# A gated block inside a two-layer kernel: the u groups computed feature-major in the wide form, the spatial product with v stationary and one group behind

## The reference

```python
def chunk_mlp_mix(h, w_in, g_v, w_s, b_s, w_out):
    bsz, length, _ = h.shape
    z = jax.nn.gelu(h @ w_in)
    u, v = jnp.split(z, 2, axis=-1)
    v = rmsnorm_2(v, g_v).reshape(bsz, length // CHUNK_2, CHUNK_2, A_GROUPS, A_WIDTH // A_GROUPS)
    s = jnp.einsum('gpq,bnqgc->bnpgc', w_s, v) + b_s.T[None, None, :, :, None]
    return (u * s.reshape(bsz, length, A_WIDTH)) @ w_out
```

## Time and profile before

| | us |
|---|---|
| median of 3 runs (2377.48 to 2377.6) | 2377.57 |
| profiled execution | 2377.55 |
| its span, first to last instruction | 2375.8 |
| TensorE busy | 2361.4 (99%) |
| VectorE busy | 1675.4 (71%) |
| ScalarE busy | 1173.7 (49%) |
| HBM read | 546 MB, 231 GB/s |

### The profile page before, as it was taken

One profiled execution on the slowest core, in us unless ns is written; L12 is line 12 of the kernel. 1 busy time (PEld: TensorE's weight loads), 2 busy tenths in 40 slices (PEclk: granted clock), 3 DMA queues, 4 the chain that ended last, 5 costly groups with the idle time before them and its releaser, 6 DMA issues.

```text
span 2375.8 us, 31444 instructions
## 1 busy us (share of the span) xinstructions
PE 2361.4 (99%) x12340; PEld 2023.3 (85%) x12340; DVE 1675.4 (71%) x2216; ACT 1173.7 (49%) x1528; POOL 0.2 (0%) x4
## 2 busy tenths in 40 slices
PE   9999999999999999999999999999999999999998
PEld 9989888888888888888888888888888888888887
DVE  6775657877877877877667777556777567765776
ACT  5443545534534534556554433446655355544554
POOL 0000000000000000000000000000000000000000
PEclk9999999999999999999999999999999999999999
DMA  7444556888888888875887887664656656566554
GB/s 265 151 161 158 206 194 254 287 285 291 283 289 288 284 283 293 283 262 187 310 286 287 288 289 271 217 207 157 197 188 192 195 186 193 188 193 191 191 183 156
DMA packets 153426, 550.44 MB, mean 232 GB/s; under 512 B 17984, under 2 KB 19776, under 8 KB 152384
## 3 DMA queue, kind: packets, MB, share of 16 engines
q1 hardware_dynamic: 152720, 548.06, 68.3%
q10 hardware_dynamic: 560, 0.36, 0.1%
HBM read 546.24 MB, written 2.11 MB: 231 GB/s over the span
## 4 chain that ended last, share of the span: by engine, by line
PE 97%; DVE 1%; DMA 1%; issue 0%; ACT 0%; DVEq 0%
PE bank L494 14%; PE bank L493 14%; PE bank L495 14%; PE mis L472 12%; PE bank L472 12%; PE mis L476 6%; PE bank L476 6%; PE mis L493 4%; PE mis L494 4%; PE mis L495 4%; PE bank L445 2%; PE bank L446 2%; PE bank L447 2%; PE mis L757 1%; DMA raw<-wstream 1%; PE mis L563 0%
## 5 line engine op out<-in xcount | busy, mean ns | idle before, releaser
L1252 DVE TENSOR_TENSOR wlo<-raw,whi 128x1024 fp32r<-128x1024 f32 x824 | 1005.3, 1223 | 624.7 <-ACT whi L840 623.3
L840 ACT ACTIVATE whi<-raw 128x1024 fp32r<-128x1024 f32 x824 | 871.1, 1060 | 1063.1 <-PE bank L495 426.2
L472 PE MATMUL mis<-xs,whi 128*128 128x512 f32 x1216 | 382.0, 395 | 0.0
L472 PE MATMUL bank<-xs,whi 128*128 128x512 f32 x1200 | 377.9, 396 | 0.0
L493 PE MATMUL bank<-whi,hs 128*128 128x512 f32 x808 | 314.6, 389 | 0.0
L494 PE MATMUL bank<-whi,hs 128*128 128x512 f32 x808 | 314.4, 389 | 0.0
L495 PE MATMUL bank<-wlo,hs 128*128 128x512 f32 x808 | 314.4, 389 | 0.0
L476 PEld LDWEIGHTS mis<-xs,wlo 128*128 128x128 f32 x1216 | 228.4, 188 | 54.0
L476 PEld LDWEIGHTS bank<-xs,wlo 128*128 128x128 f32 x1200 | 225.4, 188 | 53.3
L493 PE MATMUL bank<-whi,xs 128*128 128x512 f32 x640 | 252.9, 395 | 0.3 <-issue 0.3
L495 PE MATMUL bank<-wlo,xs 128*128 128x512 f32 x640 | 249.3, 390 | 0.0
(11 more groups left out here) (232 smaller groups left out, 2410.9 us busy)
## 6 DMA issues: line engine op xcount, KB each, us to landing
raw<-wstream SPq DMA_DIRECT2D x824, 512.0 KB, 4.4
aring<-astream SPq DMA_DIRECT2D x192, 512.0 KB, 5.0
gvb<-gvrow SPq DMA_DIRECT2D x8, 256.0 KB, 5.7
gate<-gate_rows SPq DMA_DIRECT2D x2, 1024.0 KB, 9.0
x<-xt SPq DMA_DIRECT2D x3, 512.0 KB, 8.3
out<-acc SPq DMA_DIRECT2D x2, 640.0 KB, 3.6
pw<-poolw SPq DMA_DIRECT2D x1, 1024.0 KB, 5.5
silu_c<-rows SPq DMA_DIRECT2D x1, 1024.0 KB, 7.6
```

Source lines behind the costliest of these rows:

```text
L472: pe.matmul(banks[m][:, :], whi[:, slot, c], xs[:, kt0 + k, :], start=first and k == 0, stop=False, skip_group_check=True)
L840: act.activation(whi[:, slot, :], raw[:, slot, :], ACT.Copy).then_inc(hi_ready, 1)
L1252: dve.tensor_tensor(wlo[:, slot, :], raw[:, slot, :], whi[:, slot, :].bitcast(F32), ALU.subtract).then_inc(lo_ready, 1)
```

## The change

- The u groups run in the wide form. Their sums go to `t0` (`sum_of`), the gelu is taken there in place, and the group is fed by `low_parts` and `sums_of_parts`. The first u group waits for the banks of the last v group before its third block of columns.
- The down groups of the block use banks 0 and 1 of either set (`sum_bank`).
- v is scaled by ScalarE, without the gain, at step 6 of its own group. The spatial product has v stationary and the mix matrix moving, 8 matmuls of 128 columns, behind unit 2 of the next group, into the two upper banks of its own group's set; its output has features on partitions.
- The gain is now a scalar of a partition (`gv`) and the bias a row (`bsr`, two buffers); VectorE applies both at step 3 of the next group, and multiplies by u. The transposes, `hidden_to_features`, `hidden_hi` and `hidden_lo` go. `gated_hi` stands at step 4 and `gated_lo` at step 5 of the next group.
- Left out below: the declarations of tiles and semaphores, the exchange of the inputs `gvrow`, `bsp` for `bsrow`, `gvp`, the two-line use of `freed` in `group` for (G_AU, 0), the deleted functions, `gelu_v` with both gelus ahead of both squares, `sum_of` in `sums_of_parts`, and the count of sums before the feed-forward part (H_F for H_A).

```diff
...
@@ -322,13 +323,19 @@
 def sum_bank(j, b):
-    if G_MLP <= j < G_AV or j >= G_FF:
+    if G_MLP <= j < G_AV or j >= G_AU:
         return (bank, mis)[j % 2][b]
     return bank[2 * (j % 2) + b]
+def sum_of(j, m):
+
+    if G_AU <= j < G_FF:
+        return t0[:, m // 2, (m % 2) * T:(m % 2 + 1) * T]
+    return zs[:, j % 2, m, :]
+
 def by_features(j):
-    return G_MLP <= j < G_AV or j >= G_FF
+    return G_MLP <= j < G_AV or j >= G_AU
 def evac_at(j):
@@ -358,8 +365,9 @@
     def spatial_part(g):
         sp.dma_start(ws[:, 2 * g:2 * g + 2, :], wsT[:, 2 * g:2 * g + 2, :]).then_inc(ws_arrived, 16)
-    def gv_part(g):
-        sp.dma_start(gvb[:, :], gvrow[0:1, g * NC:(g + 1) * NC].to_broadcast([P, NC])).then_inc(gv_arrived, 16)
+    def bias_rows(g):
+        sp.dma_start(bsr[:, g % 2, :], bsrow[0:1, g * 2 * P:(g + 1) * 2 * P].to_broadcast([P, 2 * P])
+                     ).then_inc(bs_arrived[g % 2], 16)
     def x_part(q):
         lo, hi = X_PARTS[q]
...
@@ -400,13 +408,14 @@
             ada(k)
         if n == (G_AV + 2) * GU:
             sp.wait_ge(xs_lo, 23)
-            gv_part(0)
+            bias_rows(0)
+            bias_rows(1)
         if G_AV < j <= G_AV + 4 and i % 4 == 2:
             spatial_part(2 * (j - G_AV - 1) + i // 4)
-        g = 4 * ((j - G_AU) // 8) + (j - G_AU) % 8
-        if G_AU <= j < G_FF and (j - G_AU) % 8 < 4 and i == 3 and g < 7:
-            sp.wait_ge(vs_ready, g + 1)
-            gv_part(g + 1)
+        for g in range(6):
+            if (j, i) == (G_AU + 8 * (g // 4) + g % 4 + 2, 3):
+                sp.wait_ge(tok_ready, 2 * g + 2)
+                bias_rows(g + 2)
         if j in (G_AU + 2, G_AU + 10) and i in (2, 4):
             h = (j - G_AU) // 8
             if i == 2:
@@ -462,11 +471,13 @@
                                skip_group_check=True)
         mm.then_inc(unit_used, 1)
-    def wide_unit(kt0, n, first, last, banks):
+    def wide_unit(kt0, n, first, last, banks, freed=None):
         pe.wait_ge(lo_ready, n + 1)
         slot = n % RING
         for m in range(MT):
+            if freed and m == 2:
+                pe.wait_ge(*freed)
             for k in range(UK):
                 c = slice(k * NC + m * P, k * NC + (m + 1) * P)
                 pe.matmul(banks[m][:, :], whi[:, slot, c], xs[:, kt0 + k, :], start=first and k == 0, stop=False,
...
@@ -748,36 +751,33 @@
         group(G_AV + g, xs, wait=normed(2), between=between, second=None if g else (tile_lo, 2),
               middle=None if g else after_first(2))
-    def spatial(g):
+    def spatial(g, j):
         pe.wait_ge(vs_ready, g + 1)
-        if g:
-            pe.wait_ge(tok_ready, g)
-        for b in range(2):
-            for s in range(2):
-                mm = pe.matmul(mis[b][:, s * T:(s + 1) * T], ws[:, 2 * g + s, :], vs[:, b, s * T:(s + 1) * T],
-                               start=True, stop=True)
+        pe.wait_ge(bank_free, 2 * j + 2)
+        for m in range(MT):
+            for b in range(2):
+                mm = pe.matmul((bank, mis)[j % 2][2 + m // 2][:, (m % 2) * T + b * P:(m % 2) * T + (b + 1) * P],
+                               vs[:, b, m * P:(m + 1) * P], ws[:, 2 * g + m // 2, :], start=True, stop=True)
         mm.then_inc(mixs_ready, 1)
     for half in range(2):
         for p in range(4):
-            g = 4 * half + p
-
-            def between(u, p=p, g=g):
+            g, j = 4 * half + p, G_AU + 8 * half + p
+
+            def between(u, p=p, g=g, j=j):
                 if u == 2 and p:
-                    pe.wait_ge(hid_lo, 2 * (H_A + g - 1))
-                    hidden_to_features(H_A + g - 1, 2)
-                if u == 4:
-                    if not g:
+                    if g == 1:
                         pe.wait_ge(ws_arrived, 16 * 8)
-                    spatial(g)
-            group(G_AU + 8 * half + p, xs, wait=normed(2), between=between)
-        for g in range(4):
-            def between(u, g=g):
-                if g == 0 and u == 2:
-                    pe.wait_ge(hid_lo, 2 * (H_A + 4 * half + 3))
-                    hidden_to_features(H_A + 4 * half + 3, 2)
-            group(G_AU + 8 * half + 4 + g, hs, wait=lambda u: (hid_lo, 2 * (H_A + 4 * half) + u + 1),
-                  between=between, by_halves=half == 1 and g == 3)
+                    spatial(g - 1, j - 1)
+            if g >= 2:
+                pe.wait_ge(gate_taken, g - 1)
+            group(j, xs, token=False, wait=normed(2), between=between)
+        for d in range(4):
+            def between(u, d=d, g=g, j=j):
+                if d == 0 and u == 2:
+                    spatial(g, j)
+            group(G_AU + 8 * half + 4 + d, hs, wait=lambda u: (hid_lo, 2 * (H_A + 4 * half) + u + 1),
+                  between=between, by_halves=half == 1 and d == 3)
     busy(15, eye)
     enter(3)
...
@@ -1070,7 +1064,7 @@
     def low_parts(j):
         act.wait_ge(unit_used, evac_at(j))
         for m in range(MT):
-            act.activation(zs[:, j % 2, m, :], (bank, mis)[j % 2][m][:, T:], ACT.Copy).then_inc(zl_ready, 1)
+            act.activation(sum_of(j, m), (bank, mis)[j % 2][m][:, T:], ACT.Copy).then_inc(zl_ready, 1)
     def hidden(j, hg, p, b):
         act.wait_ge(relu_ready, 2 * hg + b + 1)
...
@@ -1144,12 +1139,23 @@
     act.activation(rv[:, :], rv[:, :], ACT.Sqrt, bias=eps[:, :], scale=1.0 / AV).then_inc(sd_v, 1)
     def gelu_u(j, g):
-        act.wait_ge(unit_used, evac_at(j))
+        for b in range(2):
+            act.wait_ge(bank_free, 2 * j + b + 1)
+            act.activation(t0[:, b, :], t0[:, b, :], ACT.Gelu_apprx_tanh).then_inc(gelu_ready, 1)
+
+    def scaled_v(g):
+        act.wait_ge(rv_ready, 1)
         if g:
-            act.wait_ge(tok_ready, g)
-        for b in range(2):
-            act.activation(t0[:, b, :], bank[2 * (j % 2) + b][:, :], ACT.Gelu_apprx_tanh
-                           ).then_inc(bank_free, 1)
+            act.wait_ge(mixs_ready, g)
+        for b in range(2):
+            ins = act.activation(vs[:, b, :], vtok[:, b, g * NC:(g + 1) * NC], ACT.Copy, scale=rv[:, b:b + 1])
+        ins.then_inc(vs_ready, 1)
+
+    def gated_hi(g):
+        for b in range(2):
+            act.wait_ge(tok_ready, 2 * g + b + 1)
+            t = 4 * (g % 4) + 2 * b
+            act.activation(hs[:, t:t + 2, 0:T], tiles(t1[:, b, :]), ACT.Copy).then_inc(hid_hi, 1)
     def gated_squares(s, g, before):
         for b in range(2):
@@ -1160,17 +1166,24 @@
     for half in range(2):
         for p in range(4):
-            g = 4 * half + p
-            body(G_AU + 8 * half + p, lambda: gelu_u(G_AU + 8 * half + p, g),
-                 after=lambda i: hidden_hi(H_A + g - 1, 4 * (p - 1), 2) if i == 3 and p else None)
-        for g in range(4):
-            def after(i, g=g):
-                if i == 3 and g == 0:
-                    hidden_hi(H_A + 4 * half + 3, 12, 2)
-                if half and g == 3 and i == 5:
+            g, j = 4 * half + p, G_AU + 8 * half + p
+
+            def after(i, p=p, g=g):
+                if p and i == 4:
+                    gated_hi(g - 1)
+                if i == 6:
+                    scaled_v(g)
+            body(j, None, after=after)
+            low_parts(j)
+            gelu_u(j, g)
+        for d in range(4):
+            def after(i, g=g, d=d):
+                if d == 0 and i == 4:
+                    gated_hi(g)
+                if half and d == 3 and i == 5:
                     sqrt_table()
-            body(G_AU + 8 * half + 4 + g, (lambda g=g: gated_squares(S_ATT, g, 0)) if half else None,
-                 after=after, last=not (half and g == 3))
+            body(G_AU + 8 * half + 4 + d, (lambda d=d: gated_squares(S_ATT, d, 0)) if half else None,
+                 after=after, last=not (half and d == 3))
     root(S_ATT)
     split(first_unit(G_FF) + RING - 1)
     features(3, G_FF)
...
@@ -1756,28 +1762,32 @@
     dve.wait_ge(ssv_ready, 1)
     dve.tensor_reduce(rv[:, :], ssv[:, :, :], AX.X, ALU.add).then_inc(var_v, 1)
     dve.wait_ge(sd_v, 1)
-    link(dve.reciprocal(rv[:, :], rv[:, :]))
-
-    def scaled_v(g):
-        dve.wait_ge(gv_arrived, 16 * (g + 1))
-        if g:
-            dve.wait_ge(mixs_ready, g)
-        for b in range(2):
-            ins = dve.scalar_tensor_tensor(out=vs[:, b, :], in0=vtok[:, b, g * NC:(g + 1) * NC],
-                                           scalar=rv[:, b:b + 1], in1=gvb[:, :], op0=ALU.mult, op1=ALU.mult)
-        ins.then_inc(vs_ready, 1)
+    dve.reciprocal(rv[:, :], rv[:, :]).then_inc(rv_ready, 1)
     def spatial_gate(j, g):
         dve.wait_ge(mixs_ready, g + 1)
-        dve.wait_ge(tr_done, 2 * g)
-        for b in range(2):
-            dve.wait_ge(bank_free, 2 * j + b + 1)
-            for s in range(2):
-                c = slice(s * T, (s + 1) * T)
-                ins = dve.scalar_tensor_tensor(out=t1[:, b, c], in0=mis[b][:, c],
-                                               scalar=bs[:, 2 * g + s:2 * g + s + 1], in1=t0[:, b, c],
```

(97 more changed lines are left out.)

1 line of the change is left out of this document (removed).

## The result

| | before | after |
|---|---|---|
| median, us | 2377.58 | 2389.71 (2388.8 to 2390.07) |
| profiled execution, its span | 2377.55, 2375.8 | 2390.07, 2388.2 |
| TensorE busy | 2361.4 | 2364.6 |
| mean granted clock | 0.999 | 0.996 |

The changed kernel is slower by 0.47%: ratio 1.0047, 95% interval 1.0036 to 1.0057. The forecast was 2387.6, in a range of 2382.8 to 2391.0. The experiments were measured in two series, in which the kernel before has medians of 2377.8 and 2378.7 (`early_h0`, `early_h1` and `gate2_lo5` are in the second), so medians of different series agree only to about 1 us.

What follows compares the result with a forecast made beforehand. TensorE, busy 2361.4 of 2375.8 us, was taken to bound the kernel. Work -2.3, first bank +0.1, stalls +9.9 and clock +2.4 gave +10.1 us, so 2387.6 us, range 2382.8 to 2391.0.

Steps and rivals of the forecast that it cites:

- The work of TensorE: Gated block: wide form +4.2 us, transposes gone -7.0, spatial product +0.5; sum -2.3 us.
- the first bank: First u group, third block of columns: TensorE waits for the last v group's banks; +0.1 us, bounds 0 and 1.2.
- rival (D): U groups: only columns count, extra matmuls cost nearly nothing; 2383.4 us with stalls (chance 0.04), 2371.1 without (0.01).
- The stalls: First down group of each half, before unit 6: TensorE waits for VectorE's low part; 6.1 and 3.8 us, together +9.9.
- hand-made schedule: First down group, first half: splits, ada steps, gate, products and low part timed from unit 3's end; TensorE at 11.55 us.
- lower bound with free gating: First down groups: stall if the gating cost nothing; 3.4 us, 4.5 with one ada step, 7.9 together.
- Rival (C): First down groups: low parts are ready before unit 6, no stall, only the work sum remains; 2375.2 us, chance 0.08.
- The clock: Behind the stalls: granted clock falls once, after the 6.1 us stall; +2.4 us, bounds 0 and 4.8.
- rival (B): Clock falls twice behind the stalls, or weights come late in the first half as well; about 2390.3 us, chance 0.18.
- the bias rows: Issued behind a wait for tok_ready, ahead of weight loads; taken as 0, bounds 0 and 3 us for the first half.
- the additional copies and sums: Gated block: ScalarE's new copies and VectorE's sums and products fall on engines at 46% and 73%.
- the wait of the spatial product on the sums: Behind unit 2 of the next group: sums done by e+5.3, TensorE arrives at 8.4; margin 3 us, no cost.

Runs made afterwards that it cites:

- early_h0: The changed kernel with spatial_gate at step 2, gated_hi and gated_lo at step 3 in the first half's first down group only; 2381.02 us.
- early_h1: The changed kernel with spatial_gate at step 2, gated_hi and gated_lo at step 3 in the second half's first down group only; 2385.56 us.
- gate2_lo5: The changed kernel with spatial_gate at step 2 and gated_hi at step 3, gated_lo left at step 5 of the first down group; 2387.77 us.
- lo4: The changed kernel with gated_lo alone moved from step 5 to step 4 of each half's first down group; 2382.26 us.

## Why the prediction was right, and where it wasn't

**The work of TensorE: right.** Forecast -2.3 and +0.1 for the first bank. The u groups last 22.35 us (1260.45 to 1282.80, the first, without a spatial product) and 24.08 (1282.80 to 1306.88, the second), where 22.29 and 24.1 had been put together; the spatial product holds TensorE for 1.78 to 1.79 us. From the timeline of the changed kernel, the first starts of the three groups, and from its chain of waits one spatial product:

```profile
1260.45 0.62 PE L483 MATMUL bank<-xs,whi 128*128 128x512 f32 x2
...
1282.80 0.63 PE L483 MATMUL mis<-xs,whi 128*128 128x512 f32 x2
...
1306.88 0.63 PE L483 MATMUL bank<-xs,whi 128*128 128x512 f32 x2
```

```profile
1291.33 1.78 PE bank L759 x16
```

With the stalls gone, the block is 2.4 us shorter than before. The rival (D), by which only columns count, is out: the wide form kept its pace of the earlier trace rows, 22.35 us for the first group where D gives 21.76 (32 sets of 0.680).

**The stalls: right in place, order and size.** Forecast 6.1 and 3.8, measured 5.9 and 3.6. In the first half every step of the hand-made schedule from the gate on is in the timeline above (unit 4 started at 1367.75, which is its 0), in the order put down, and within 0.3 us of its place. The lower bound with free gating, 4.5 and 3.4, has its own measurement: 4.2 and 3.1 us of idle time with the gate early, which with some 0.2 us between idle time and the distance of starts is that bound. Rival (C), no stall, was decided at the point named: once the low part no longer stood behind split 5 and the gating came one step earlier, the kernel took 2375.8, against 2375.2 for that rival.

**The clock: right in kind, one fall too few.** The step that failed is "a stall of 6.1 is past 4.1, one of 3.8 just short of it. I take one fall". It took the one fall that the trace of before shows for a threshold. After the change the clock fell twice, and cost 1.8 + 2.9 = 4.7 us in place of 2.4, at the far end of the bounds given (0 to 4.8). That is the first half of rival (B); its second half, late weights, didn't come: no wait of TensorE names `wlo`. This term is the largest part of the difference between forecast and result. The others nearly cancel: the stalls 0.5 shorter and the work 0.2 less than forecast, against 0.8 us ahead of the block. So the result is nearer to rival (B)'s 2390.3, which had 0.18, than to the forecast. The size of a fall, 2.4, was taken from the kernel's start, and the two falls of the changed kernel cost 1.8 and 2.9; that their mean, 2.35, is so near it is luck.

**What was hidden stayed hidden.** Nothing was visible of the bias rows, the additional copies and sums, or the wait of the spatial product on the sums: TensorE is busy for all of 96.90 us in the first u groups, with VectorE at 76% and ScalarE at 57%.

The sum over the block, -2.4 + 9.4 + 4.7 = 11.7, is what its two ends in the profiles show; the remaining 0.8 us of the profiled execution's difference lie ahead of the block, which starts at 1260.45 in place of 1259.69.

## What to carry to other kernels

When work is moved between steps of an engine's queue, look at what the step stands behind: an entry is as late as the latest thing that the entries before it wait for, here a ring slot freed by the very unit whose successor needs the entry's result. The first test is one line: the consumer waits before unit k, so the producer may stand behind nothing that waits for unit k-1. It isn't enough: `lo4` passes it and still waits 4.5 us, so the producer's whole chain has to be added up as well, with the splits that stand in it. And a stall of a few us of a TensorE that is the bound has a second price behind it, the clock's, here half of the first (4.7 to 9.4 us); if the stall can't be avoided, matmuls whose result isn't used took nearly all of that second price away here (4.3 of 4.7 us).

## What the runs showed of the hardware

The granted clock fell at very different times after the last matmul: 4.1 us at the end of the kernel before, 2.3 us in the changed kernel's first stall (matmul's end 1373.35, clock 0.84 in the microsecond from 1375, 0.50 behind it) and 2.5 in the second (end 1564.35; table by stages, clock third from the end of the line):

```profile
1375.00:1376.00 1.00, 0.00 (x0) 0.00 (x0) 0.51 (x1) 0.98 (x2) 0.00 (x0) 0.84 0.08 29
1376.00:1377.00 1.00, 0.00 (x0) 0.00 (x0) 0.99 (x1) 0.00 (x0) 0.00 (x0) 0.50 0.50 78
...
1566.00:1567.00 1.00, 0.00 (x0) 0.00 (x0) 1.00 (x1) 0.00 (x0) 0.00 (x0) 0.92 0.51 102
1567.00:1568.00 1.00, 0.26 (x1) 0.26 (x2) 1.00 (x3) 0.00 (x0) 0.00 (x0) 0.50 1.02 410
```

In the kernel before with its low part at step 5, the clock fell only when TensorE had been back at work for about 1.5 us, behind an idle time of 3.07 (0.88 in the microsecond from 1571, 0.50 behind it; timeline of TensorE, starts 0.23 apart, then 0.43):

```profile
1570.30 0.50 PE L493 MATMUL bank<-whi,hs 128*128 128x512 f32 x1 [3.07 <-DVE hs L1377]
1570.64 0.39 PE L494 MATMUL bank<-whi,hs 128*128 128x512 f32 x1
1570.87 0.39 PE L495 MATMUL bank<-wlo,hs 128*128 128x512 f32 x1
1571.10 0.40 PE L493 MATMUL bank<-whi,hs 128*128 128x512 f32 x1
...
1571.81 0.63 PE L493 MATMUL bank<-whi,hs 128*128 128x512 f32 x1
1572.23 0.63 PE L494 MATMUL bank<-whi,hs 128*128 128x512 f32 x1
```

Behind the two shorter stalls of `lo4`, 2.8 and 1.7 us, the clock stayed at 1.00 in the trace. Where it fell, the stretch at 1.2 GHz behind the stall lasted 3.2 to 3.5 us in five cases and 5.4 to 6.1 in three. So the same stall has a price that differs from execution to execution.

The start of the kernel has such a fall too, in some executions. The wait for `x` there went from 0.2 to 2.7 us between profiles. In the five with 1.2 us or less the clock reads 1.00 through the first 40 us; in the four with 1.6 or more it reads 0.50 for some microseconds between 7 and 16. From `early_h1`, the wait and two microseconds behind it:

```profile
PE mis L575 <- DMA x<-xt: 2.7, 1, 2.7
...
8.00:9.00 1.00, 0.76 (x4) 0.79 (x5) 0.00 (x0) 0.00 (x0) 0.00 (x0) 0.50 1.02 364
9.00:10.00 1.00, 1.00 (x6) 0.79 (x4) 0.00 (x0) 0.56 (x2) 0.00 (x0) 0.50 1.05 404
```

In these four the block starts 1.6 to 2.8 us later than in the kernel before, in the other five 0 to 0.8. Wait and fall go together here; nothing was varied to show that one causes the other. A delay of 1.6 to 2.8 us is nearly as much as the runs of one kernel scatter: 3.8 us over the ten of `early_h0`, but also 3.1 over 21 of the kernel before, which has no stall. So the scatter of the runs can't be put down to the stalls, and the lengths of the block are what the experiments should be compared by.
